# Expert weights of a two-layer decoder trunk loaded in pieces of 1 MiB through eighteen ring places instead of 2 MiB through nine

## What is computed

```python
for i in range(DEPTH):                       # 2 layers
    h = h + mixer(rms_norm(h, norm_mix[i]))
    h = h + hierarchical_moe(rms_norm(h, norm_ffn[i]), ...)
return rms_norm(h, final_norm)

def expert_block(args):                      # each of 32 experts, on the tokens routed to it
    xb, e = args
    g, u = jnp.split(xb @ w_gate_up[e], 2, axis=-1)   # w_gate_up[e]: 1024 x 1024
    return (jax.nn.silu(g) * u) @ w_down[e]           # w_down[e]:     512 x 1024
```

## Time and profile before

| | us |
|---|---|
| median of 3 runs | 1341.86 (1341.44 to 1343.41) |
| the profiled execution's own time | 1341.31 |
| its span in the trace | 1339.6 |
| PE busy | 1281.9 (96%) |
| DVE busy | 498.7 (37%) |
| ACT busy | 311.7 (23%) |
| POOL busy | 148.9 (11%) |
| bytes moved by DMA | 462.53 MB |

### The profile page before, as it was taken

The page is one execution under the profiler, slowest core; times in us unless marked ns, Lnnn a source line. Parts: engine busy times, 40 slices in busy tenths (PEclk is TensorE's granted clock), DMA queues, the critical chain, the costliest instruction groups (busy, mean ns, idle before and its releaser), DMA issues.

```text
span 1339.6 us, 15996 instructions
## 1 busy us (share of the span) xinstructions
PE 1281.9 (96%) x6188; PEld 687.6 (51%) x6188; DVE 498.7 (37%) x1178; ACT 311.7 (23%) x622; POOL 148.9 (11%) x122
## 2 busy tenths in 40 slices
PE   7999999999999998989999999999999999999896
PEld 5777664444444433334588888744444444433342
DVE  5586342223222322224656662432223222322235
ACT  3267611111111111111443321211111111111103
POOL 4950120000000000000000002200001000000000
PEclk9999989999999999999999999899999999999999
DMA  9901569999999999999823336689999999999997
GB/s 347 342 8 60 255 259 419 429 427 428 429 427 429 428 428 426 428 427 426 257 88 105 103 142 267 250 347 427 427 428 428 427 428 428 429 426 428 426 428 296
DMA packets 68579, 462.53 MB, mean 345 GB/s; under 512 B 18020, under 2 KB 33406, under 8 KB 43956
## 3 DMA queue, kind: packets, MB, share of 16 engines
q1 hardware_dynamic: 63232, 452.87, 81.6%
q0 software_dynamic: 4800, 7.96, 1.6%
q10 hardware_dynamic: 500, 1.06, 0.2%
HBM read 443.40 MB, written 26.24 MB: 351 GB/s over the span
## 4 chain that ended last, share of the span: by engine, by line
PE 75%; DMA 21%; DVE 2%; ACT 0%; issue 0%; SPq 0%; POOLq 0%; DVEq 0%
PE ps L1170 22%; PE ps L962 20%; PE ps L1188 13%; DMA big<-in_moe_w_gate_up_dram 12%; PE ps L1145 8%; DMA small<-in_moe_w_gate_up_dram 6%; DMA big<-rows 2%; PE ps L1160 2%; PE ps L1179 1%; PE ps L926 1%; PE ps L1105 1%; PE ps L1271 1%; PE ps L1154 1%; PE ps L1044 1%; PE ps L1011 1%; PE ps L945 1%
## 5 line engine op out<-in xcount | busy, mean ns | idle before, releaser
L1170 PE MATMUL ps<-big,arena 128*64 128x512 f32 x976 | 218.2, 594 | 17.1 <-DMA big<-in_moe_w_gate_up_dram 15.6
L1685 DVE SCALAR_TENSOR_TENSOR gain<-ps,slot_root,arena 64x512 f32<-64x512 f32 x64 | 72.8, 1137 | 403.1 <-ACT arena L810 402.1
L617 POOL DMA_INDIRECT rows<-arena x60 | 59.0, 983 | 827.7 <-DVE arena L1713 827.7
L1170 PEld LDWEIGHTS ps<-big,arena 128*64 128x64 f32 x976 | 68.9, 137 | 158.4 <-issue 131.1
L810 ACT ACTIVATE arena<-ps,slot_root 64x512 f32<-64x512 f32 x64 | 43.7, 682 | 452.6 <-PE ps L1170 452.6
L1170 PE MATMUL ps<-small,arena 128*64 128x512 f32 x496 | 111.9, 593 | 5.1 <-DMA small<-in_moe_w_gate_up_dram 5.1
L962 PE MATMUL ps<-xt_parts,small_parts 128*128 128x512 f32 x288 | 110.6, 393 | 0.0
L962 PE MATMUL ps<-xr_parts,small_parts 128*128 128x512 f32 x272 | 105.9, 389 | 0.0
L1188 PE MATMUL ps<-big,arena 128*64 128x512 f32 x432 | 98.7, 598 | 1.5 <-DMA big<-in_moe_w_down_dram 1.5
L962 PE MATMUL ps<-xt_parts,big_parts 128*128 128x512 f32 x256 | 99.7, 389 | 0.0
L1170 PEld LDWEIGHTS ps<-small,arena 128*64 128x64 f32 x496 | 35.4, 137 | 77.0 <-issue 68.3
(11 more groups left out here) (218 smaller groups left out, 1687.7 us busy)
## 6 DMA issues: line engine op xcount, KB each, us to landing
big<-in_moe_w_gate_up_dram SPq DMA_DIRECT2D x61, 2048.0 KB, 27.9
small<-in_moe_w_gate_up_dram SPq DMA_DIRECT2D x31, 2048.0 KB, 28.6
big<-in_moe_w_down_dram SPq DMA_DIRECT2D x27, 2048.0 KB, 30.1
arena<-in_moe_w_gate_up_dram SPq DMA_DIRECT2D x16, 2048.0 KB, 30.1
small<-in_moe_w_down_dram SPq DMA_DIRECT2D x11, 2048.0 KB, 28.7
xt<-in_moe_w_gate_up_dram SPq DMA_DIRECT2D x10, 2048.0 KB, 25.4
h<-in_moe_w_gate_up_dram SPq DMA_DIRECT2D x10, 2048.0 KB, 24.7
xt<-in_moe_w_down_dram SPq DMA_DIRECT2D x10, 2048.0 KB, 31.8
```

Source lines behind the costliest of these rows:

```text
L617: nc.gpsimd.indirect_dma_start(out=rows_dram[l], out_offset=bass.IndirectOffsetOnAxis(ap=where[:, j:j + 1], axis=0), in_=S.y_rows[:, j, :] ...
L1170: mm = nc.tensor.matmul(ps[2 + j][half * BLOCK:(half + 1) * BLOCK, :], S.xg[:, k, j * BLOCK:(j + 1) * BLOCK], w[:, a, half * FF:(half + 1) ...
L1685: V.scalar_tensor_tensor(out=hid[BLOCK:P, j, :].rearrange("q (k p) -> q p k", p=P), in0=ps[2 + j][BLOCK:P, :].rearrange("q (p k) -> q p k" ...
```

## The change

`PIECES` becomes 12, `RING` becomes 18, and a piece is `PIECE = 2` rows of 4 KB in a partition, that is 8 KB, 1 MiB for each DMA. Each of the nine places is cut into two, so the memory is the same and so is the order of the bytes. SP issues 192 loads for each layer instead of 96; from the nineteenth on each waits for the release of the half piece 18 before it. PE waits for each half piece and releases each half piece, so `gate_up` is called four times for each expert and `down` twice; the matmuls and their order are the same. Every wait on `gu_done` or `down_done` elsewhere counts twice as many. Nine semaphores that were used once at the start (`x_in`, `rel_in`, `query_in`, `w_o_in`, `kv_in`, `bo_in`) are now the semaphores of the ring places 9 to 17, whose waits in the expert stage count one load more.

```diff
-    PIECES = 6
-    RING = 9
+    PIECES = 12
+    PIECE = 2
+    RING = 18
...
+        FIRST_IN = RING // 2
+        x_in = ring_in[FIRST_IN:FIRST_IN + TT]
+        rel_in, query_in, w_o_in, kv_in, bo_in = ring_in[FIRST_IN + TT:]
...
-        ring = [[halves[1][0], small[:, 0], halves[0][1], halves[0][0], late_slot, halves[1][1], small[:, 1], xt_slot, h[:]],
-                [*halves[1], halves[0][0], late_slot, small[:, 1], halves[0][1], small[:, 0], xt_slot, h[:]]]
+        places = [[halves[1][0], small[:, 0], halves[0][1], halves[0][0], late_slot, halves[1][1], small[:, 1], xt_slot, h[:]],
+                  [*halves[1], halves[0][0], late_slot, small[:, 1], halves[0][1], small[:, 0], xt_slot, h[:]]]
+        ring = [[place[:, at:at + PIECE] for place in of_layer for at in range(0, FT, PIECE)] for of_layer in places]
...
             at = q * PIECES + c
-            eng.wait_ge(ring_in[at % RING], m * (GROUP * PIECES // RING * 16)
-                        + (at // RING + 1 + l * -(-(PAIRS * PIECES - at % RING) // RING)) * 16)
+            s = at % RING
+            eng.wait_ge(ring_in[s], m * (GROUP * PIECES // RING * 16)
+                        + (at // RING + 1 + (s >= FIRST_IN) + l * -(-(PAIRS * PIECES - s) // RING)) * 16)
...
                         else:
                             before, used = divmod(n - RING, PIECES)
-                            if used < 4:
-                                sp.wait_ge(main[l].gu_done, 4 * before + used + 1)
+                            if used < 8:
+                                sp.wait_ge(main[l].gu_done, 8 * before + used + 1)
                             else:
-                                sp.wait_ge(main[l].down_done, 2 * before + used - 4 + 1)
-                        if c < 4:
-                            w = w_gate_up[l, 2 * i + c // 2].rearrange("(p k) n -> p k n", p=P)[:, c % 2 * FT:(c % 2 + 1) * FT]
+                                sp.wait_ge(main[l].down_done, 4 * before + used - 8 + 1)
+                        if c < 8:
+                            w, part = w_gate_up[l, 2 * i + c // 4], c % 4
                         else:
-                            w = w_down[l, 2 * i + c - 4].rearrange("(p k) n -> p k n", p=P)
+                            w, part = w_down[l, 2 * i + (c - 8) // 2], c % 2
+                        w = w.rearrange("(p k) n -> p k n", p=P)[:, part * PIECE:(part + 1) * PIECE]
                         sp.dma_start(ring[l][n % RING], w).then_inc(ring_in[n % RING], 16)
...
             def gate_up(S, j, part, w):
 
-                for a in range(FT):
-                    k = part * FT + a
+                for a in range(PIECE):
+                    k = part * PIECE + a
...
                 def up(m, q, j):
+                    for part in range(4):
+                        if j == 0 and part % 2 == 0:
+                            pe.wait_ge(S.rows_taken, (m * GROUP + q) * 4 + part // 2 + 3)
+                        ring_loaded(pe, l, m, q, 4 * j + part)
+                        gate_up(S, j, part, slot(q, 4 * j + part))
+
+                def finish(m, q, j):
                     for part in range(2):
-                        if j == 0:
-                            pe.wait_ge(S.rows_taken, (m * GROUP + q) * 4 + part + 3)
-                        ring_loaded(pe, l, m, q, 2 * j + part)
-                        gate_up(S, j, part, slot(q, 2 * j + part))
-
-                def finish(m, q, j):
-                    ring_loaded(pe, l, m, q, 4 + j)
-                    down(S, (m * GROUP + q) * 2 + j, j, slot(q, 4 + j))
+                        ring_loaded(pe, l, m, q, 8 + 2 * j + part)
+                        down(S, (m * GROUP + q) * 2 + j, j, part, slot(q, 8 + 2 * j + part))
```

More of the change, by code:

```diff
@@ L210, in build_trunk @@
         assert L == 2 and T == 512 and D == 1024 and HG == 8 and KV == 2
-        x_in = [sem(f"x_in{t}") for t in range(TT)]
         cleared = sem("cleared")
@@ L228, in build_trunk @@
         attn_in = sem("attn_in")
-        rel_in = sem("rel_in")
         conv_in = [sem(f"conv_in{b}") for b in range(2)]
@@ L323, in build_trunk @@
         xt_slot = xt[:].rearrange("p (a b) c -> p a (b c)", a=FT)
-        ring = [[halves[1][0], small[:, 0], halves[0][1], halves[0][0], late_slot, halves[1][1], small[:, 1], xt_slot, h[:]],
-                [*halves[1], halves[0][0], late_slot, small[:, 1], halves[0][1], small[:, 0], xt_slot, h[:]]]
+        places = [[halves[1][0], small[:, 0], halves[0][1], halves[0][0], late_slot, halves[1][1], small[:, 1], xt_slot, h[:]],
+                  [*halves[1], halves[0][0], late_slot, small[:, 1], halves[0][1], small[:, 0], xt_slot, h[:]]]
+        ring = [[place[:, at:at + PIECE] for place in of_layer for at in range(0, FT, PIECE)] for of_layer in places]
         def stage(l, t):
-            return ring[l][t // 2][:, t % 2 * 2:t % 2 * 2 + 2, :]
+            return ring[l][t]
         PE_ROWS = 2
@@ L439, in load_experts_over @@
                                         "a (p k) n -> p (a k) n", p=P)).then_inc(over_in[l], 16)
-                            sp.wait_ge(over[l].down_done, r * E)
+                            sp.wait_ge(over[l].down_done, r * (2 * E))
                             sp.sem_inc(sp_mark, 1)
@@ L464, in load_experts @@
                         n = i * PIECES + c
-                        if n == RING - 1:
+                        if n // 2 == RING // 2 - 1:
                             sp.wait_ge(x_split, TT * (l + 1))
@@ L468, in load_experts @@
                         elif n < RING:
[L469 removed]
+                            sp.wait_ge(*early_free[n // 2])
                         else:
                             before, used = divmod(n - RING, PIECES)
[L472 to L479 removed]
+                            if used < 8:
+                                sp.wait_ge(main[l].gu_done, 8 * before + used + 1)
+                            else:
+                                sp.wait_ge(main[l].down_done, 4 * before + used - 8 + 1)
+                        if c < 8:
+                            w, part = w_gate_up[l, 2 * i + c // 4], c % 4
+                        else:
+                            w, part = w_down[l, 2 * i + (c - 8) // 2], c % 2
+                        w = w.rearrange("(p k) n -> p k n", p=P)[:, part * PIECE:(part + 1) * PIECE]
                         sp.dma_start(ring[l][n % RING], w).then_inc(ring_in[n % RING], 16)
             def load_rows(l):
[L484 removed]
+                sp.wait_ge(main[l].gu_done, 8 * LAST + 4)
                 for j in range(2):
@@ L536, in _ @@
                 if q < BIG_SLOTS:
-                    sp.wait_ge(main[0].gu_done, 2 * E)
+                    sp.wait_ge(main[0].gu_done, 4 * E)
                 else:
@@ L808, in swish @@
                 act.wait_ge(S.where_ready, i + 1)
-                act.wait_ge(S.gu_done, i * 4 + j * 2 + 2)
+                act.wait_ge(S.gu_done, i * 8 + j * 4 + 4)
                 nc.scalar.activation(S.silu[BLOCK:P, j, :], ps[2 + j][0:BLOCK, :], ACT.Silu,
@@ L834, in experts @@
                 act.wait_ge(S.gathered, 3 * PAIRS + 1)
-                act.wait_ge(S.gu_done, 4 * PAIRS)
+                act.wait_ge(S.gu_done, 8 * PAIRS)
                 for j in range(2):
@@ L840, in experts @@
                 for j in range(2):
-                    act.wait_ge(S.down_done, 2 * LAST + j + 1)
+                    act.wait_ge(S.down_done, 4 * LAST + 2 * j + 2)
                     act.wait_ge(S.scattered[j], 16 * LAST)
@@ L891, in _ @@
             act.wait_ge(conv_in[0], 16 * 3)
-            act.wait_ge(main[0].down_done, 2 * LAST + 1)
+            act.wait_ge(main[0].down_done, 4 * LAST + 2)
             split_high_of(0, [0])
@@ L1181, in turn_hidden, with down @@
                 mm.then_inc(S.turned, 1)
-            def down(S, n, j, w):
-                pe.wait_ge(S.hidT_ready, n + 1)
-                for k in range(FT):
+            def down(S, n, j, part, w):
+                if part == 0:
+                    pe.wait_ge(S.hidT_ready, n + 1)
+                for a in range(PIECE):
+                    k = part * PIECE + a
                     for half in range(2):
                         mm = nc.tensor.matmul(ps[6 + j][half * BLOCK:(half + 1) * BLOCK, :], hidT[:, j, k, :],
-                                              w[:, k, half * HALF:(half + 1) * HALF],
+                                              w[:, a, half * HALF:(half + 1) * HALF],
                                               start=(k == 0), stop=(k == FT - 1))
@@ L1295, in experts @@
                                 for j in range(2):
-                                    for part in range(2):
-                                        gate_up(over[l], j, part, halves[j][part])
+                                    for part in range(4):
+                                        gate_up(over[l], j, part, big[:, j, part * PIECE:(part + 1) * PIECE])
                                 for j in range(2):
```

(5 more changed lines are left out.)

## The result

The changed kernel takes 1352.46 us (median of 4 runs, 1350.63 to 1353.66) against 1341.65 us (median of 4) for the kernel before: ratio 1.0082, 95% interval 1.0064 to 1.0100. It is 10.8 us slower. Forecast were 1348.7 us and +6.8 us, with a range of 1343.5 to 1353.5.

A forecast was written before the change was run, and what follows sets the result against it. Saturated DMA was taken to bound the expert stages from restart to last byte. Per layer, +5.1 us for packets less 1.7 us for the restart gave +3.4, +6.8 in two layers: 1348.7 us, range 1343.5 to 1353.5.

The forecast's parts named there:

- What bounds the kernel: Expert stages: DMA is saturated from its restart to the last byte, 427 to 428 GB/s, 30.2 us a pair.
- Smaller packets: Weight loads: 8 KB instead of 16 KB runs, 783 more packets per layer at 6.5 ns, +5.1 us a layer.
- Earlier restart: After the standstill in each layer: first release after 8 matmuls instead of 16, DMA restarts 1.7 us earlier.
- Twice the waits on PE: Expert stage: six more waits a pair, at most 0.2 us each, 1.2 us a pair, covered by the DMA's pace.
- the cover of 3 us a pair: Expert stage: PE needs 27.1 us a pair, the DMA 30.2, so PE's added waits stay hidden.
- Twice the issues on SP: SP's weight loads: an issue takes 0.33 us against 2.5 us between half pieces, so hidden.
- The last half piece: Layer's end: PE needs 1.8 instead of 3.65 us after the last landing, worth nothing because DVE adds the row tile later.
- the tail unchanged: Layer's end: time from the last weights to the end stays the same, set by the row tile landing 2.5 us later.
- Packets cost less: Rival on weight packets: 0.5 to 4 ns each, sum -2.6 to +2.9 us, about 1342 us; chance 0.14.
- faster: Rival: earlier restart with packet cost near zero, visible only below 0.5 ns, -3.4 us, 1338.5 us; chance 0.07.
- A pause for each DMA: Rival: engines stand still, say 0.1 us, at each DMA boundary, 1366 us; chance 0.05 together with PE as bound.
- PE becomes the bound: Rival in the expert stages: each added wait costs PE 0.5 us or more; chance 0.05 together with a DMA pause.

The follow-up runs named there:

- the even and odd DMAs: Kernel before, every 2 MiB piece loaded by two DMAs of 64 partitions, even and odd ones, 16 KB packets kept: 1339.83 us against 1340.62, ratio 1.0003.
- the second comparison: The changed kernel itself measured once more against the kernel before: 1353.6 us (4 runs) against 1339.98, ratio 1.0113 (1.0095 to 1.0130).

## Why the prediction was right, point by point

**What bounds the kernel: right.** The DMA engines are full from the restart to the end of a layer, and whatever changes their rate comes out at the end: 428, 421 and 410 GB/s give 0, +12.7 and +38.1 us.

**Smaller packets: right in kind, too small in size.** The term "783 for each layer, x 6.5 ns = 5.1 us" is the one that was off. The rates over 440 to 600 us say 16 engines x 16384 B x (1/421 - 1/428) = 10 ns for one packet more, and (1/410 - 1/428) = 26.9 ns for three more, 9.0 each; the times say 9.1 ns with 8 KB and with 4 KB packets. The pace is 30.7 us a pair, where 424 to 425 GB/s and 30.5 to 30.6 us were forecast. 2 x 783 x 9.1 = 14.3 us instead of 10.2. If the added end marks cost nothing, which the even and odd DMAs allow, it is 2 x 696 x 9.1 = 12.7 us. The two readings it was put between, 5.2 and 7.4 ns, came from 6 to 7 us of the `w_out` load against a stretch of 431 GB/s without scatters. That the stretch had no scatters is not the reason: over 206 to 221 us, also without them, the same working gives 8.6 ns with 8 KB and 9.4 ns with 4 KB weight packets. Why the load of `w_out` shows less is open. The value from the 1 KB packets, 9.8 ns, which I had put down as the upper bound, was the better one. In the restart-to-tile stretch of the profiles the term measures 6.4 and 7.3 us (8.8 ns for each of 783 packets), with what the earlier restart loses again in it. The Trainium skill gives about 3 cycles a packet in "DMA: Bandwidth & Descriptors", section "Why small descriptors are slow". The estimate from it, 3.5 ns, is well under what these runs show.

**Earlier restart: right in time, a little less in worth.** The issue is 1.9 us earlier (1.7 after the 0.2 us by which the gate and up matmuls start earlier). Alone it brought 2.4 us in two layers, not 3.4. 14.3 - 2.4 = 11.9 us (10.3 with free end marks) against 10.8 and, in the second comparison, 15.1 us measured (13.6 by the medians): the interval of each comparison is about 5 us wide, so the parts agree with the whole only so far.

**Twice the waits on PE: right.** PE is as full in the first half of a layer as before (220.00 of 220 us), so the cover of 3 us a pair holds. From its first gate and up matmul to the end of the last expert layer 0 takes PE 451.6 us instead of 448.6, the 3 us more of idle time that were forecast.

**Twice the issues on SP: wrong in the number, right in the outcome.** An issue was put at 0.33 us; from about 340 us on in layer 0 and 1020 us in layer 1 it takes some 2.1 us, about the time that the engines need for one DMA. It hides all the same: the engines' share stays at 1.01. The kernel with 8 KB packets in 2 MiB DMAs has the same blocking, and so has the same end.

**The last half piece worth nothing, the tail unchanged: right as far as the row tile goes.** The tile still ends the stretch in both layers. What follows it in layer 0 was no term of the sum: the combine starts later and runs longer, about 2 us in the profile. More slack for PE was called harmless, and no run shows that it was not: with the same slack, the kernel without the earlier restart has neither the longer idle time nor the deeper fall of the clock.

**Rivals.** "Packets cost less" and "faster" needed under 4 and 0.5 ns; measured are 9. "A pause for each DMA" is excluded by the even and odd DMAs (1.0003), "PE becomes the bound" by PE's waits for weights in the second half.

**The number.** The measured loss is 4.0 us over the forecast of +6.8 in the first comparison and 8.3 us over it in the second (6.8 by the medians). The larger loss from packets (+4.1 us, or +2.5 with free end marks), the 1 us less from the restart and the 2 us in the combine make 5.5 to 7.1 us, between the two; single terms can't be checked closer than that. Some luck is in it: 1352.5 lies in the range, but near its end, and the loss of the second comparison would lie beyond it. The upper bound was also drawn a little short: 9.8 ns a packet, +12.0 us, on the median of 1341.86 is 1353.9 and not 1353.5.

## What to carry to other kernels

Where the DMA engines are full, count packets and not DMAs: the contiguous run in a partition sets their number, and here each costs 9 ns of its engine beyond its bytes, 1.5% for 8 KB against 16 KB runs. Finer pieces paid only where the queue was empty, at the first release after a standstill: the two kernels that split that one reload and nothing else, in halves and in quarters, are the only ones whose interval lies below 1, with ratios of 0.9982 (0.9970 to 0.9993) and 0.9984 (0.9973 to 0.9995), against 0.82% lost by splitting all. And when PE is idle in front of critical work, compare where the wait ends with the result that it is said to wait for, before filling it: here PE started 1.0 and 1.5 us after that result.

## What the runs showed that I had not expected

- **DMAs over 64 neighbouring partitions can run at half the rate.** 218 GB/s at a DMA share of 1.01 in the profiled execution, against 427 GB/s when the two DMAs of a piece take even and odd partitions. The engines count as busy in both, so the share alone does not show it; only GB/s does. One execution of six took 1821.69 us and not 2112 to 2203, so it isn't always half; the cause was not tested.
- **SP's issues get long when many packets are in flight.** From about 400 us on in layer 0 an issue takes 0.33 us with 2 MiB in 16 KB packets, 2.1 us with 1 MiB in 8 KB packets and 4.6 to 4.9 us with 2 MiB in 8 KB packets, the last two about one DMA's time on the engines (2.5 and 5.0 us). With two DMAs of 1 MiB in 16 KB packets two issues take 1.1 us together. The median time to landing over 440 to 600 us, divided by a DMA's time and multiplied by its packets per engine, is an estimate of the packets in flight: 65 and 60 per engine in the two kernels with 16 KB packets, 90 and 105 in the two with 8 KB, some 150 with 4 KB. So there is no one count at which an issue blocks, and what fills up is open.
- **PE's idle time before the combine of layer 0.** Its end goes with a packet of the instruction queue, 2.7 to 2.9 us before, and in the changed kernel's two profiles not with DVE's result. After 5.0 and 5.5 us of idle the granted clock was 0.77 over 15 us, after 2.2 to 2.4 us it was 0.89 or 1.00, and where matmuls on the identity stand in between and 0.5 us or less is left, 1.00.
